# Collecting a group's rows already turned: 24 small products in place of 6 wide ones and 8 transposes

## The reference

```python
def _hier_moe(xn, w_rg, b_rg, w_re, b_re, w_gate, w_up, w_down):
    t = xn.reshape(-1, D_MODEL)
    ...            # the top group, then the top 2 of its 8 experts, and their weights -> combine
    y = jnp.zeros_like(t)
    for g in range(N_GROUPS):                       # 4 groups of 8 experts, D_EXPERT = 256
        hid = jax.nn.silu(jnp.einsum('nd,edf->nef', t, w_gate[g])) * jnp.einsum('nd,edf->nef', t, w_up[g])
        y = y + jnp.einsum('nef,efd->nd', hid * combine[:, g, :, None], w_down[g])
    return y.reshape(shp)
```

## Time and profile before

| what | value |
|---|---|
| median of 3 runs | 667.61 us (667.5 to 670.08) |
| the profiled execution's own time | 666.25 us |
| its span, first to last instruction | 664.4 us |
| PE busy | 562.7 us, 85% of the span |
| weight loads of PE | 317.7 us, 48% |
| DVE busy | 371.5 us, 56% |
| ACT busy | 136.2 us, 20% |
| mean granted clock of TensorE | 0.935 |
| HBM read | 208.76 MB |

### The profile page before, as it was taken

The page is one execution under the profiler, slowest core; times in us unless marked ns, Lnnn a source line. Parts: engine busy times, 40 slices in busy tenths (PEclk is TensorE's granted clock), DMA queues, the critical chain, the costliest instruction groups (busy, mean ns, idle before and its releaser), DMA issues.

```text
span 664.4 us, 7517 instructions
## 1 busy us (share of the span) xinstructions
PE 562.7 (85%) x2900; PEld 317.7 (48%) x2900; DVE 371.5 (56%) x679; ACT 136.2 (20%) x267; POOL 129.8 (20%) x116
## 2 busy tenths in 40 slices
PE   3998889989999467988979997797998989788882
PEld 1775567877888424446468445332322323222220
DVE  4069999999999998820423144734342442414124
ACT  3013401115211144451610021110101111010102
POOL 1625441111111877772000000000000000000001
PEclk9999989999999567985999999798999999999997
DMA  8999768798874948999469983469999999999951
GB/s 311 398 357 334 288 235 325 291 402 299 289 281 133 378 153 314 422 423 394 172 163 408 384 340 106 148 220 417 419 420 418 421 420 421 420 420 421 407 233 68
DMA packets 66318, 213.83 MB, mean 322 GB/s; under 512 B 15379, under 2 KB 17955, under 8 KB 58092
## 3 DMA queue, kind: packets, MB, share of 16 engines
q1 hardware_dynamic: 52108, 137.46, 53.2%
q0 software_dynamic: 11392, 73.41, 28.8%
q10 hardware_dynamic: 2784, 2.51, 1.1%
HBM read 208.76 MB, written 4.60 MB: 321 GB/s over the span
## 4 chain that ended last, share of the span: by engine, by line
PE 44%; DVE 24%; SPq 10%; DMA 7%; ACT 6%; issue 5%; POOL 3%; ACTq 1%; DVEq 0%
PE PS L619 7%; SPq L469 7%; DVE arena L1734 6%; PE PS L1185 6%; DVE x_rows L1738 6%; PE PS L1167 5%; PE PS L1080 4%; PE PS L1095 4%; PE PS L1193 3%; DMA arena<-in_w_down 3%; SPq L474 3%; PE PS L1233 3%; DMA arena<-in_w_up 2%; POOL arena L549 2%; POOL temp L549 1%
## 5 line engine op out<-in xcount | busy, mean ns | idle before, releaser
L619 PE MATMUL PS<-xT,arena 128*128 128x264 f32 x608 | 145.6, 399 | 0.8 <-ACT arena L1376 0.5
L619 PEld LDWEIGHTS PS<-xT,arena 128*128 128x128 f32 x608 | 116.8, 195 | 26.4 <-issue 4.7
L1734 DVE TENSOR_TENSOR arena<-arena,x_rows 128x2048 f32<-128x2048 f32 x32 | 73.1, 2283 | 21.2 <-ACT x_rows L1328 21.1
L1738 DVE TENSOR_REDUCE x_rows<-arena 128x32 f32<-128x2048 f32 x32 | 73.2, 2287 | 1.1
L549 POOL DMA_INDIRECT arena<-in_cache_k_b,unit_idx x32 | 44.6, 1395 | 138.9 <-DVE x_rows L1738 134.5
L1193 PE MATMUL PS<-temp 128*128 128x512 f32 (+1 forms) x96 | 48.9, 646 | 12.4 <-DVE temp L2261 8.1
L1185 PE MATMUL PS<-arena,temp 128*32 128x512 f32 x384 | 48.0, 644 | 9.3 <-DMA arena<-in_w_up 4.8
L609 POOL TENSOR_TENSOR small<-small,consts 128x1 f32<-128x1 f32 x3 | 2.6, 868 | 241.2 <-DVE small L2297 241.2
L2237 DVE TENSOR_TENSOR x_rows<-PS,x_rows 128x512 f32<-128x512 f32 (+1 forms) x48 | 32.9, 687 | 24.4 <-PE PS L1193 24.3
L549 POOL DMA_INDIRECT arena<-in_cache_v_b,unit_idx x32 | 34.9, 1090 | 29.6 <-PE PS L1025 13.4
L2261 DVE COPY temp<-PS 128x512 f32<-128x512 f32 x8 | 5.5, 691 | 55.1 <-PE PS L1233 55.1
(11 more groups left out here) (374 smaller groups left out, 804.2 us busy)
## 6 DMA issues: line engine op xcount, KB each, us to landing
arena<-in_w_down SPq DMA_DIRECT2D x32, 1024.0 KB, 15.9
arena<-in_w_gate SPq DMA_DIRECT2D x48, 512.0 KB, 13.1
arena<-in_w_up SPq DMA_DIRECT2D x48, 512.0 KB, 13.6
arena<-in_w_in SPq DMA_DIRECT2D x9, 2048.0 KB, 11.3
temp<-in_w_gate SPq DMA_DIRECT2D x12, 512.0 KB, 14.8
temp<-in_w_up SPq DMA_DIRECT2D x12, 512.0 KB, 14.7
temp<-in_w_out SPq DMA_DIRECT2D x1, 4096.0 KB, 15.3
x_rows<-in_x_prompt SPq DMA_DIRECT2D x2, 1024.0 KB
```

The source lines that it names most:

```text
L619: last = nc.tensor.matmul(PS[0:m, n % 2, 0:T], w[:, k, c0:c0 + m], xT[:, k, :], start=(k == 0), stop=(k == KC - 1))
L1734: nc.vector.tensor_tensor(k_ring[:, u], k_ring[:, u], q_all[:, b % 2:b % 2 + 1, :].to_broadcast([P, 4, H * HD]), ALU.mult).then_inc(s_mul, 1)
L1738: nc.vector.tensor_reduce(z_s[:, b, :].rearrange("p (h r) -> p r h", r=R)[:, 4 * u:4 * u + 4, :], k_ring[:, u].rearrange("p r (h d) -> p r ...
```

## The change

`collect` now takes the activations as the fixed operand (every eighth column, d, d+8, ..., of a row tile: 128 columns) and moves the selection `into` (128 columns) past them. For each of 8 slices d there are three products, of 128, 128 and 8 rows, and the result is already turned: model width on the partitions, slots along the row. `turn` and `xg` go. ACT copies bank 0 (slices 0 to 3) to the first half of `xgT`, DVE bank 1 (slices 4 to 7) to the second; `begin` waits for ACT's copy, and a new wait on DVE's stands ahead of the next `collect`. DVE's copy moves behind its product of hid.

```diff
             def collect(i):
                 for half in range(2):
-                    for t, (_, n) in enumerate(TILES):
-                        if half == 0:
-                            pe.wait_ge(s_into, i * 3 + (t + 1))
-                        last = nc.tensor.matmul(PS[:, half, :], into[0:n, t, :], x2_rows[t][0:n, half * 512:(half + 1) * 512],
-                                                start=(t == 0), stop=(t == 2))
+                    for d in range(4 * half, 4 * half + 4):
+                        for t, (_, n) in enumerate(TILES):
+                            if d == 0:
+                                pe.wait_ge(s_into, i * 3 + (t + 1))
+                            last = nc.tensor.matmul(PS[:, half, d % 4 * QUAD:(d % 4 + 1) * QUAD],
+                                                    x2_rows[t][0:n, d:D:KC], into[0:n, t, :],
+                                                    start=(t == 0), stop=(t == 2))
                     last.then_inc(s_xg, 1)
-
-            def turn(i):
-
-                pe.wait_ge(s_xg0, i + 1)
-                pe.wait_ge(s_xg1, i + 1)
-                for c in range(KC):
-                    last = nc.tensor.transpose(PS[:, c // 4, c % 4 * QUAD:(c % 4 + 1) * QUAD],
-                                               xg.rearrange("p h n -> p (h n)")[:, c:D:KC], ident)
-                last.then_inc(s_gtr, 1)
...
@@ PE, quad
                 turn_back(i)
+                pe.wait_ge(s_xg1, i + 1)
                 collect(i + 1)
                 pe.wait_ge(s_second, i * 128 + 128)
                 gate_up(1).then_inc(s_gu, 1)
-                turn(i + 1)
                 turn_hid(i)
...
             collect(0)
-            turn(0)
             begin(0, 0, 0)
...
@@ ACT
             def collected(i):
                 act.wait_ge(s_xg, i * 2 + 1)
-                nc.scalar.copy(xg[:, 0, :], PS[:, 0, :]).then_inc(s_xg0, 1)
-
-            def turned(i):
-                act.wait_ge(s_gtr, i + 1)
-                nc.scalar.copy(xgT.rearrange("p (b c) n -> p b (c n)", b=2), PS[:, 0:2, :]).then_inc(s_gT, 1)
+                nc.scalar.copy(xgT[:, 0:4, :].rearrange("p c n -> p (c n)"), PS[:, 0, :]).then_inc(s_gT, 1)
...
@@ DVE
             def collected(i):
                 dve.wait_ge(s_xg, i * 2 + 2)
-                nc.vector.tensor_copy(xg[:, 1, :], PS[:, 1, :]).then_inc(s_xg1, 1)
+                nc.vector.tensor_copy(xgT[:, 4:8, :].rearrange("p c n -> p (c n)"), PS[:, 1, :]).then_inc(s_xg1, 1)
...
                     slots_back(i + 1)
-                    collected(i + 1)
                 dve.wait_ge(s_act, i + 1)
                 nc.vector.tensor_tensor(hid, PS[:, 2, DE:2 * DE], act_e, ALU.mult).then_inc(s_hid, 1)
                 if ahead:
+                    collected(i + 1)
                     next_slots(i + 2)
```

More of the change, by code:

```diff
@@ L316, in decoder_step @@
         y_sb = temp[:, 9216:9216 + D].rearrange("p (h n) -> p h n", h=2)
-        xg = temp[:, 10240:10240 + D].rearrange("p (h n) -> p h n", h=2)
         flat = rows_kva.rearrange("p t n -> p (t n)")
@@ L372, in decoder_step @@
         s_step = sem("s_step")
-        s_xg, s_xg0, s_xg1, s_half = sem("s_xg"), sem("s_xg0"), sem("s_xg1"), sem("s_half")
-        s_gtr, s_gT, s_gu, s_gexp2, s_act, s_hid, s_hT, s_hTc, s_down, s_y0, s_y1 = (sem(n) for n in (
-            "s_gtr", "s_gT", "s_gu", "s_gexp2", "s_act", "s_hid", "s_hT", "s_hTc", "s_down", "s_y0", "s_y1"))
+        s_xg, s_xg1, s_half = sem("s_xg"), sem("s_xg1"), sem("s_half")
+        s_gT, s_gu, s_gexp2, s_act, s_hid, s_hT, s_hTc, s_down, s_y0, s_y1 = (sem(n) for n in (
+            "s_gT", "s_gu", "s_gexp2", "s_act", "s_hid", "s_hT", "s_hTc", "s_down", "s_y0", "s_y1"))
         s_comb, s_add, s_fcomb, s_fadd = (sem(n) for n in ("s_comb", "s_add", "s_fcomb", "s_fadd"))
@@ L1279, in overflow @@
                 collect(t)
-                turn(t)
                 begin(t, 0, t - NQ // 2)
@@ L1628, in quad @@
                 nc.scalar.activation(act_e, PS[:, 2, 0:DE], ACT.Silu).then_inc(s_act, 1)
-                if ahead:
-                    turned(i + 1)
-                else:
+                if not ahead:
                     returning(i)
@@ L1639, in _ @@
             collected(0)
-            turned(0)
             act.preload_act_table(ACT.Silu)
@@ L1650, in overflow @@
                 collected(t)
-                turned(t)
                 quad(t, False)
```

## The result

The changed kernel takes 743.45 us (median of 4 runs, 739.88 to 744.21), the kernel before 667.56 us beside it: a ratio of 1.113 (95% interval 1.107 to 1.118). I had said 669.3 us, at most 677.0. The profiled execution has a span of 742.4 us against 664.4.

A forecast was written before the change was run, and what follows sets the result against it. Weight transfers, about 30 us a quad against 26.35 of PE, were taken to bound most of the stage. Collects +2.49 us, hid path -0.57 and an earlier start left +1.7 after slack: 669.3 us, range 665.4 to 677.0.

The forecast's parts named there:

- The stride of the loads: Collect's weight loads, one column in 8: taken to cost nothing, with 48 ns or a doubling per load kept for the range.
- the stride rival: Each of collect's 48 strided loads takes longer: collect 10.7 or 13.6 us, 688 to 711 us in all; chance 0.20.
- The switches: In collect, 16 switches between 128 and 8 rows instead of 4, about 0.195 us each: 8.42 us, +2.49 per collect.
- The start: collect(0) to begin(0): clock rises at 424.0, collect ends at 430.8, begin(0) at 434.4, 2.1 us earlier than before.
- The rival at 676.0: Clock rival: granted clock stays low to the end of collect(0), costing 6.7 us there; the clock rival's chance was 0.17.
- The path through hid: From gate_up's end to begin, without the eight transposes and xgT copy ahead of hid's copy: 0.57 us shorter.
- DVE's moved copy: Second-half copy placed behind the product of hid: costed at nothing, or 0.1 to 0.4 us if its cover is gone.
- The slack at the gates: Gates at 476.71 and 617.13 (gate_up ends that restart transfers) may come 1.9 and 1.4 us later before DMA idles.
- What I held untouched: Everything after the last w_down landing, at 642.16 in the kernel before, was taken as unchanged.

The follow-up runs named there:

- the kernel with contiguous ones: Kernel before, with the stride of 8 elements moved from the turn's weight loads to the collect's moving operand: 731.29 us in one run, ratio 1.071.
- the two wide ones: Sixth and eighth collects of the changed kernel with products streaming the selection twice (256 columns) where the next PSUM columns are begun afterwards: ratio 1.155.
- the contiguous kernel: Changed kernel with each slice's weights 128 neighbouring columns of x2_rows instead of every eighth; results are other numbers: 676.42 us, ratio 1.012.
- the third one: Changed kernel with x2_rows written permuted for contiguous loads and the row tile as outer loop, 4 switches per collect: 663.62 us, ratio 0.9944.
- the one without short products: Slice-by-slice collect with contiguous loads, each slice's 8-row product replaced by a second 128-row one; results are other numbers: 679.91 us in one run, ratio 0.995.
- the same 16-switch kernels: Changed kernel with contiguous loads, 676.42 us; and with permuted activations and 256-column products where possible in collect(0) alone, 694.47 us in one run.

## Why the prediction was wrong

**The stride of the loads: the step that failed.** I wrote "I take nothing, because the strided load and L985's last the same". I compared the durations of two different kinds of load, 193 ns for a strided one of a transpose and 187 for a contiguous one of a two-pass product, and took their likeness as a common rate. But the duration of a load is not its pace: contiguous two-pass loads last 187 to 192 ns and follow each other after 0.11 us, so about 80 ns of each are overlapped. Taking these 80 off, I estimate the loads of the earlier trace rows at 60 ns for a contiguous transpose and 113 for a strided one: the stride had nearly doubled it there already (the first two loads of a turn start 0.09 us apart with the stride and, in the kernel with contiguous ones, 0.06). It did not show because a transpose streams for 0.11 us and hides a load of that length. A two-pass load that is at 0.11 us already has no such room: with the stride it took 0.237, and a collect 15.6 us instead of 8.42. So the row that I cited against the rival was for it. The Trainium skill's rule of a penalty where each read finds another 16-byte line, "Advanced Engine Details and Errata", section Memory Cachelines, which I set against my forecast, was right. The like-for-like comparison (L1176 with L1103, both transposes) should have carried the chance; it had 0.20.

**The size of the stride rival.** It was bounded at 711 us, and the time is 743.45. Three terms were short. The load is 0.237 us and not the doubled 0.214: 8 x 1.81 = 14.5 us for a collect at the full clock instead of 13.6. The clock falls inside the collect, 15.65 - 14.5 = some 1.2 us. And gate_up(1) behind it starts at the half clock: 1.7 us more. I had the clock as a rival of the start only, and not as something that comes with slow loads in every quad. Together 15.65 + 5.3 against 13.6 + 3.57, 3.8 us in each of seven quads, 26 us, and 3.9 us at the start (begin(0) ending at 443.54, not 434.4 + 5.2), of the 32 us between 711 and 743. The split of the 15.65 us between stride and clock is worked out from the two paces within one collect, and collect(0), all at 0.50, bears it out with 16.25 us. No run had this collect at the full clock throughout; the two wide ones of 15.8 us that kept it stream more.

**The switches: right.** 16 of 0.195 us, a collect of 8.42; 8.44 without the stride (15 of them inside, and what I counted as the sixteenth is the entry and the end of the group). What the +2.49 us for each collect does to the end came out a little worse than I had it. In the contiguous kernel the five quads between the gates at 484.71 and 627.41 take 28.54 us each (28.25 forecast), 1.5 us in all.

**The start: wrong way.** I said begin(0) would end 2.1 us earlier, at 434.4. In the changed kernel it ends at 443.54, in the contiguous one at 440.02. I let the clock rise at 424.0 since it did so in the earlier trace rows, though the products under it were others. The rival at 676.0 carried just this, with 0.17, and the contiguous kernel landed on it with 676.42; its parts differ a little (collect(0) 15.03 and not 16.8 us, begin(0) 4.44 and not 3.57).

**The path through hid: right.** From the gate at 464.80 to begin(1) at 466.62 are 1.82 us in the changed kernel, 1.9 forecast, 2.47 before. All engines in order of time:

```profile
464.82 0.38 ACT L1615 ACTIVATE temp<-PS 128x256 f32<-128x256 f32 x1 [12.57 <-PE PS L1177]
...
465.72 0.44 PE L1210 MATMUL PS<-consts,temp 128*128 128x128 f32 x2 [0.97 <-DVE temp L2239]
...
466.19 0.37 ACT L1619 COPY temp<-PS 128x256 f32<-128x256 f32 x1 [0.99 <-PE PS L1210]
```

The copy of hid starts right behind the two transposes, and DVE's moved copy, L2203, lies beside them (0.68 us from 465.58). It cost nothing, as I took it.

**The slack at the gates: not found.** I read slack into a first transfer that landed 1.4 us later than one on an idle queue, and gave the last gate 1.4 us of it. In the contiguous kernel this gate comes at 627.41 and the last w_down lands at 652.27 (633.40 + 18.87): 10.3 and 10.1 us later than in the kernel before, so next to nothing was absorbed.

**What I held untouched: the last down product.** I wrote that everything after the last landing is untouched. The chain of the kernel before, where the level is 1.00, and of the changed kernel:

```profile
642.30 3.67 PE PS L1233 x32
```

```profile
718.71 5.29 PE PS L1225 x32
```

In the changed kernel the level is 0.50 there until 722.0. The contiguous kernel (5.33 us) and the third one (5.37) have the same, but not the one without short products (3.67). Why the level is low there isn't shown; the 1.6 us are.

**The agreement with 676.0 is in part luck.** That rival wanted a landing 8.4 us later and nothing behind it. The contiguous kernel has 10.1 us and 1.6 more, for the slack that wasn't there, 1.5 us in the quads and the last down product, less a start that was 1.1 us cheaper than the rival had it (begin(0) ending at 440.0 and not at 437.5 + 3.57). So its profiled span is 11.7 us longer, and its median 8.9.

## What to carry to other kernels

Before a strided operand replaces a contiguous one on TensorE, look at how far its elements lie apart in bytes, and compare like with like: the distance between the starts of two loads of the same kind, not their durations. Here 16 bytes or more between f32 elements doubled a weight read, 32 bytes doubled that of the moving operand, and writing the data once in the order of its eight readers cost 0.36 us for 512 columns. When an idea is right but slow, separate its parts: turned collection with a permuted write and the row tile outside is 0.6% faster than the kernel before, and what the change gains in its trace comes from the start alone, since the transfers set the pace later.

## What the runs showed of the hardware that I had not expected

- TensorE reads f32 at about 1.8 ns an element when each lies 16 or 32 bytes from the last as weights (0.237 us for 128), or 32 as moving data (0.92 us for 512). With 4 or 8 bytes from one to the next, loads follow after 0.108 to 0.118 us. The slow pace is about the same at both levels of the clock (0.235 to 0.240 us in collect(0) of the changed kernel, all at 0.50).
- With a strided weight read the clock falls although the profile has PE busy for all of the time: in the changed kernel to 0.50 some 5 us into each collect that began at 1.00, with the loads 0.24 us apart, against 1.00 throughout with the loads 0.11 us apart. It isn't certain to: two wide collects with the same loads kept 1.00 for all of their 15.8 us.
- 48 instructions of 128 columns stay at 0.50 for 15.03 us if every third pair has 8 rows, and for 22.7 us when most of them stream 256 columns. With the short pairs gathered in two groups, or made 128 rows high, the level rises after 3.2 to 3.9 us. In the later collects of the same 16-switch kernels the level was 1.00 at the start, and it stayed there: the same instructions hold either level. That the level at the start decides it is argued only, since the transfers beside them differ too (a DMA share of 0.94 in collect(1), 0.00 in most of collect(0)).
- DVE's product takes 1.04 us instead of 0.69 for 512 columns when it writes each f32 512 bytes from the last.
